# State space layer: the turned-back states are added in pairs on VectorE, and TensorE takes two products with the output tables for each pair of groups and half in place of four

## The reference

```python
a = exp((lam_re + i lam_im) * dt)              # per group (64) and state (64)
bu = einsum('sgc,gpc->sgp', u, b_bar)          # u: 1024 tokens, 64 groups, 16 channels
h[s] = a * h[s - 1] + bu[s]                    # complex, an associative scan over the tokens
y = einsum('sgp,gcp->sgc', h_re, c_re) - einsum('sgp,gcp->sgc', h_im, c_im)
y = gelu(y + d_skip * u)
mix = (glu(y @ w_glu)) @ w_out
```

## Time and profile before

| | |
|---|---|
| time, median of 3 runs | 3222.91 us (3220.38 to 3223.18) |
| the profiled execution, its own time | 3220.77 us |
| its span | 3219.0 us |
| granted TensorE clock, mean | 0.996 |
| share of the span busy: PE, PEld, DVE, ACT, POOL | 98%, 85%, 64%, 33%, 44% |
| from VectorE's first instruction of `turned(0)` to the next stage's first transpose | 952.67 to 1080.44 us |

### The profile page before, as it was taken

One profiled execution on the slowest core, in us unless ns is written; L12 is line 12 of the kernel. 1 busy time (PEld: TensorE's weight loads), 2 busy tenths in 40 slices (PEclk: granted clock), 3 DMA queues, 4 the chain that ended last, 5 costly groups with the idle time before them and its releaser, 6 DMA issues.

```text
span 3219.0 us, 52392 instructions
## 1 busy us (share of the span) xinstructions
PE 3145.1 (98%) x19570; PEld 2742.7 (85%) x19570; DVE 2044.2 (64%) x3811; ACT 1054.8 (33%) x2049; POOL 1417.5 (44%) x1185
## 2 busy tenths in 40 slices
PE   8999999989999999999999999999999999999998
PEld 8898989979998888878888888988889888888886
DVE  4757575755679312487777775555553777777766
ACT  3545454541123211232222221544341422222221
POOL 5434344423249233665555544411104755555533
PEclk9999999999999999999999999999999999999999
DMA  7211102052101211111111111000003011111111
GB/s 196 76 55 45 60 28 69 22 190 70 50 4 21 61 41 51 66 53 52 52 52 52 52 52 62 8 20 17 14 12 105 27 53 52 52 52 52 52 51 54
DMA packets 180105, 173.35 MB, mean 54 GB/s; under 512 B 50043, under 2 KB 162875, under 8 KB 179771
## 3 DMA queue, kind: packets, MB, share of 16 engines
q1 hardware_dynamic: 179838, 170.72, 16.8%
q10 hardware_dynamic: 96, 0.26, 0.0%
HBM read 156.97 MB, written 19.23 MB: 55 GB/s over the span
## 4 chain that ended last, share of the span: by engine, by line
PE 62%; DVE 2%; ACT 1%; issue 1%; POOL 1%; POOLq 0%; DVEq 0%; ACTq 0%
PE banks L2602 16%; PE banks L78 13%; PE banks L80 13%; PE banks L79 13%; PE banks L3419 2%; PE banks L3396 1%; PE banks L214 1%; PE banks L3353 0%; PE banks L3354 0%; POOL x L182 0%; PE banks L3335 0%; PE banks L3362 0%; POOL rstd L177 0%; ACT x L198 0%; PE banks L2229 0%
## 5 line engine op out<-in xcount | busy, mean ns | idle before, releaser
L2839 DVE TENSOR_TENSOR x<-x,banks 128x512 f32<-128x512 f32 x784 | 521.8, 687 | 240.2 <-PE banks L2602 230.3
L78 PE MATMUL banks<-winbuf_hi,xt_hi 128*128 128x256 f32 x1024 | 302.5, 295 | 12.2 <-ACT qkn L920 5.4
L80 PE MATMUL banks<-winbuf_hi,xt_lo 128*128 128x256 f32 x1024 | 290.4, 284 | 0.0
L79 PE MATMUL banks<-winbuf_lo,xt_hi 128*128 128x256 f32 x1024 | 290.3, 283 | 0.0
L78 PEld LDWEIGHTS banks<-winbuf_hi,xt_hi 128*128 128x128 f32 x1024 | 196.4, 192 | 33.3 <-issue 16.0
L78 PE MATMUL banks<-h1t_hi,f1w_buf_hi 128*128 128x512 f32 x512 | 199.5, 390 | 1.6 <-issue 1.6
L78 PE MATMUL banks<-h3t_hi,f2w_buf_hi 128*128 128x512 f32 x512 | 199.4, 390 | 1.6 <-issue 1.6
L80 PE MATMUL banks<-h1t_hi,f1w_buf_lo 128*128 128x512 f32 x512 | 199.2, 389 | 0.0
L80 PE MATMUL banks<-h3t_hi,f2w_buf_lo 128*128 128x512 f32 x512 | 199.2, 389 | 0.0
L79 PE MATMUL banks<-h3t_lo,f2w_buf_hi 128*128 128x512 f32 x512 | 199.2, 389 | 0.0
L79 PE MATMUL banks<-h1t_lo,f1w_buf_hi 128*128 128x512 f32 x512 | 199.2, 389 | 0.0
(11 more groups left out here) (544 smaller groups left out, 9433.1 us busy)
## 6 DMA issues: line engine op xcount, KB each, us to landing
f1w_raw<-in_w_ff SPq DMA_DIRECT2D x32, 1024.0 KB, 5.1
f2w_raw<-in_w_ff SPq DMA_DIRECT2D x32, 1024.0 KB, 5.0
winraw<-in_w_in SPq DMA_DIRECT2D x128, 128.0 KB, 3.3
gluw_raw<-in_ssm_w_glu SPq DMA_DIRECT2D x14, 512.0 KB, 4.4
x<-in_x SPq DMA_DIRECT2D x8, 512.0 KB, 6.5
wow_raw<-in_w_out SPq DMA_DIRECT2D x4, 1024.0 KB, 6.1
x<-in_x SPq DMA_DIRECT2D x1, 4096.0 KB, 15.8
gew_raw<-in_w_ple_gate SPq DMA_DIRECT2D x4, 1024.0 KB, 4.9
```

Of the source, the lines that this page charges most:

```text
L78: nc.tensor.matmul(out, a.hi, b.hi, start=start, stop=False)
L79: nc.tensor.matmul(out, a.hi, b.lo, start=False, stop=False)
L80: return nc.tensor.matmul(out, a.lo, b.hi, start=False, stop=stop)
L2839: nc.vector.tensor_tensor(xx, xx, chip.ps[:, 4 + 2 * (p % 2) + g, :], ALU.add).then_inc(s_acc, 1)
```

## The change

`turned_back` gets two more instructions: once the four products are written, `hs[0] = hs[0] + hs[1]` and `hs[2] = hs[2] + hs[3]`, in place, and then waits for these. `outputs` takes `hs[0]` with `q[0]` and `hs[2]` with `q[1]`, two products for each half in place of four. The semaphore `s_h` now counts six for each block, and its waiters' numbers follow.

```diff
                 if b == NB - 2:
-                    sp.wait_ge(s_h, 4 * (NB // 2))
+                    sp.wait_ge(s_h, 6 * (NB // 2))
                     then.load_ahead(sp)
...
-            then.split_ahead(pool, (s_h, 4 * NB))
+            then.split_ahead(pool, (s_h, 6 * NB))
...
-                pe.wait_ge(s_h, 4 * b + 4)
+                pe.wait_ge(s_h, 6 * b + 6)
...
-                    for n in range(4):
+                    for c in range(2):
                         for h in range(2):
                             rows = slice(NST * h, NST * h + NST)
-                            last = nc.tensor.matmul(outs[h], hs[n][rows, a, :],
-                                                    q[b % 3][n // 2][rows, a, 1:n1, :].rearrange("p j c -> p (j c)"),
-                                                    start=False, stop=n == 3)
+                            last = nc.tensor.matmul(outs[h], hs[2 * c][rows, a, :],
+                                                    q[b % 3][c][rows, a, 1:n1, :].rearrange("p j c -> p (j c)"),
+                                                    start=False, stop=c == 1)
...
                 nc.vector.scalar_tensor_tensor(out[3], h1, -1.0, r0, ALU.mult, ALU.mult).then_inc(s_h, 1)
-                dve.wait_ge(s_h, 4 * b + 4)
+                dve.wait_ge(s_h, 6 * b + 4)
+                for c in range(2):
+                    nc.vector.tensor_tensor(out[2 * c], out[2 * c], out[2 * c + 1], ALU.add).then_inc(s_h, 1)
+                dve.wait_ge(s_h, 6 * b + 6)
```

## The result

| | before | after |
|---|---|---|
| median of 15 runs each | 3222.18 us (3220.06 to 3225.03) | 3238.32 us (3228.77 to 3242.26) |
| ratio of after to before | | 1.0047, 95% interval 1.0040 to 1.0054 |
| the profiled execution, its own time, span | 3220.77, 3219.0 us | 3242.26, 3240.5 us |

The change makes the kernel 16 us slower. Its runs also lie 13.5 us apart, against 5.0 before, and the mean granted clock of a run goes with its time: 0.992 in the two shortest, 0.988 to 0.989 in the seven longest (one run of 3236.1 us is listed at 0.941 and doesn't fit; I can't say why). A difference of 0.004 over 3230 us is, by estimate, 13 us of TensorE's full-speed work. The profiled execution is the slowest of the fifteen, so its stretches show what the change can cost, not its median.

What follows compares the result with a forecast made beforehand. The prediction took VectorE and TensorE as level, with VectorE setting the pace after the change. +9.7 us up to T5 and -2.5 behind it gave +7.2 us, forecast 3230.1 us, range 3223.5 to 3239.

Steps and rivals of the forecast that it cites:

- The bound: In the stage's blocks VectorE and TensorE are level now; with the adds VectorE sets the pace, at least 16.8 us per block.
- T5: The end of `turned_back(5)`, 1045.1 before the change; forecast to move by +9.7 us, with bounds 7.9 and 18.6.
- The adds: Two more VectorE adds per block: 1.3 us at rest, 3.1 us with both in collision with GpSimd.
- the sum: +9.7 us up to T5 and -2.5 us behind it: +7.2 us on the profiled 3220.8.
- the second rival: Every add collides with GpSimd: T5 moves by 18.6 us, less 2.5, giving 3239.0; chance 0.13.
- I take half of that as won back: First two blocks: all four adds collide, 3.6 us; half is won back when GpSimd runs into its waits.
- The clock: TensorE pauses ahead of each `outputs`; 3.4 us at half level costs 1.7 us, counted only ahead of `outputs(7)`.
- In blocks 0 to 4 VectorE's next ten microseconds hide it: The 1.7 us of TensorE work lost to the half clock behind each pause costs nothing in these blocks.
- From T5 to the end: From T5 to the end of `outputs(7)`: 28.1 us, 2.5 less than now.
- The signs: Wrong if VectorE waits for TensorE in blocks 1 to 4, these grow under 1.3 or over 3.1 us, or time moves behind the stage.
- the third rival: Clock down through the last blocks: `outputs(5)` and `outputs(6)` take 8.5 us each; +12.3 us, 3235.2; chance 0.10.

Runs made afterwards that it cites:

- e2: The changed kernel without the two adds on VectorE, two products in place of four (output differs); 3219.94 us, ratio 0.9995.
- e4: The kernel before with GpSimd's table products left out from block 2 and block 3 on (output differs); 3221.62 us, ratio 1.0001.
- e1: The changed kernel with identity matmuls on TensorE ahead of each `outputs`, before its wait for the states; 3232.89 us, ratio 1.0039.
- e6: e1 with fewer identity matmuls, none ahead of `outputs(5)` and `outputs(6)`; 3231.43 us, ratio 1.0029.
- e7: The changed kernel with no large VectorE instruction reading two SBUF inputs, TensorE reordered, 18 identity matmuls ahead of the last `outputs`; 3220.80 us, ratio 0.9997.
- e5: The changed kernel with the same GpSimd table products left out as in e4 (output differs); 3220.66 us, ratio 0.9993.
- e9: e7 with `kernels(b + 1)` moved ahead of `in_matrix(b + 2)` on TensorE; 3219.28 us, ratio 0.9990.
- e10: e5 with 20 identity matmuls in place of 10 ahead of the last `outputs`; 3215.52 us, ratio 0.9986.

## Why the prediction was right in sign and short in size

**The bound.** Right. VectorE set the pace up to T5, shown by e2: half the products off TensorE moved T5 by 0.02 us. And TensorE was level with it, shown by e4. `outputs` at full clock took 5.15 us for the 5.1 predicted, 256 records at L2001.

**The adds.** Near in price: 1.28 us at rest (1.3 predicted; the 7.9 of the sum is six times the unrounded 1.32), at most 3.57 in collision (3.1). The six pairs up to T5 took 3.09, 3.57, 1.28, 2.88, 2.13 and 1.28 us, 14.2 together, yet VectorE was busy for only 99.75 - 90.32 = 9.4 us more: 4.8 came back from other instructions, as forecast, and 9.4 is near the 9.7 of the sum. But that agreement leans on its idle time and is partly luck. In e1, where it waited for no `outputs` up to T5, it was busy for 11.2 us more: twelve adds at 0.64 are 7.7 us, so 3.5 us of added collisions there, where I had 1.8. The argument behind it, that GpSimd's fixed number of instructions bounds them, held against the second rival (T5 moved by 11.8 to 14.0 us in the four profiles with adds and GpSimd at work, never by 18.6), but "I take half of that as won back" was a guess, and too hopeful. This is the smaller of the two steps that failed: T5 came 12.0 us later in e1 with the clock at 1.00, 2.3 more than the 9.7 of the sum.

**The clock.** This is the larger step that failed: "In blocks 0 to 4 VectorE's next ten microseconds hide it", and a single 1.7 us at the end. I had taken the one half-level stretch of the kernel before, 3.4 us, as the size of each. It was one draw: e2 had 10 us behind a pause of the same length. In the changed kernel the half level lasts for the whole of `outputs(1)`, `(4)` and `(7)`, which then take 9.2 us and not 6.8. That is longer than VectorE's way from its second add to the end of its next scan (8.7 us in block 2, 6.8 in block 5), so the cover was gone: 0.73 and 2.66 us of waits up to T5, 1.0 in block 6, 2.4 more than allowed for in the last `outputs`, 1.8 in the identity matmuls behind it and about 1.2 in the next stage. Together 9.8 us in this execution, the slowest of the runs; of the 3.4 up to T5, 1.8 would otherwise have gone into collisions, as e1 suggests (101.5 against 99.75 us busy). Over the medians the clock is worth 16.1 - 11.5 = 4.6 us by e1, or 16.1 - 9.8 = 6.3 by e6, and both are rough: e1's identity matmuls held TensorE up behind T5 (29.5 us for e6's 27.6), and e6 still had a fall.

Not all of the miss is the clock's. Without its 1.7 us the forecast is 9.7 - 4.2 = +5.5. With the clock at 1.00 e1 took 12.0 us more up to T5 and e6 3.0 less behind it, +9.0 together. So, as an estimate from these two executions, of the 16.1 - 7.2 = 8.9 us that the forecast fell short 3.5 belong to the other terms and 5.4 to the clock, which cost about 7 in place of 1.7.

**From T5 to the end.** Predicted -2.5 us, +1.0 measured; nearly all of the difference is the clock's (1.0 and 2.4 us above). In e6, with the clock up there, it was 27.6 - 30.6 = -3.0, where the sum without the clock has -4.2: in e6 VectorE still waited 0.6 us for `outputs(5)`, and the last `outputs` waited for its copies until 11.2 us into block 7 and not 10.6.

**The signs.** Two that I had named for being wrong came. VectorE waited for TensorE in block 2 (0.73 us), and blocks 1 to 4 grew by 3.60, 0.35, 2.18 and 1.16 us, three of them outside 1.3 to 3.1. In block 2 the adds ran at rest (1.28 us), so little was added; GpSimd stood idle for 2.87 us at its end. T5 came 105.4 us after `turned(0)`, where the forecast had 92.5 + 9.7 = 102.2.

**The rivals.** The measured median, 3238.3, lies on the number of the second rival (every add collides, 3239.0), but not by its mechanism, since T5 didn't move as far. What happened is somewhat more than the forecast's adds, plus most of the third rival, which had 3235.2 and a chance of 0.10. Its reasoning was right that `outputs` at the half level for its full length holds VectorE up, and I spoke against it with a pause of 2.20 us behind which nothing fell, too little evidence for pauses of 3 to 6 us. The rule of the Trainium skill, page "TensorE: Matmul & The Clock Gate", section "Part 1: The HAM clock gate", that the clock falls to half in pauses and comes back with sustained work, agrees with the trace in direction: the falls at `outputs(0)`, `(1)`, `(4)` and `(7)` each stand behind a pause of 3.0 to 6.0 us. But not every such pause is followed by one: e7's of 3.75 us wasn't. That a VectorE instruction with two inputs in SBUF contends with GpSimd's reads, over ports that are an exclusive lock, as the Trainium skill's page "SBUF — State Buffer", section "Who interferes with whom", has it, agrees too: 0.68 us with an input in PSUM, up to 1.9 with both in SBUF.

## What to carry to other kernels

When two engines are level, taking work off one gains nothing (e2), and a pause opens on it. On TensorE such a pause can cost more than the work that was taken away: 5.3 us behind one of 3.04 in e5. So list the pauses that an edit opens, and don't size the clock's fall by the only one that the trace of before shows. Price a new VectorE instruction by whether both its inputs are in SBUF while GpSimd works: here 1.3 us or 3.6 for the same two adds. Results that are written back into a PSUM bank in place cost the same (0.70 us) and keep VectorE clear of GpSimd, but the bank comes free later, and TensorE's order has to follow.

## What the runs showed of the hardware that I had not expected

A stretch at the half level isn't one of 3.4 us only: in the changed kernel a whole `outputs` of 9.2 us ran at it, three times in one stage. The runs of the same program then differ: 13.5 us between fifteen runs, 5.0 before the change, the longer ones at a lower mean clock.

The same pause can have different ends. Behind 2.84 us the kernel before stayed at the half level for 3.4 us, behind 2.85 us e2 stayed there for about 10. Behind 3.75 us e7 stayed at the full level, behind 3.76 us at the same place e9 fell.

Identity matmuls ahead of a wait don't secure the clock (e6's fall behind a pause of 1.66 us), though ten of them at the right place were worth 5 us (e5 against e10).

The scans write to PSUM in the 2.6 us that they take to SBUF, and a product written in place in PSUM took 0.70 us.
